# The sample group's part moved from the first to the third group of blocks, with the start reordered

## The chip, the cores and the metric

The kernel runs on one core of a Trainium2 chip. The metric is device time in microseconds (us) of one execution, the median of three runs. A core has five engines that run their own instruction streams and meet at semaphores: TensorE (PE; PEld is its weight load), VectorE (DVE), ScalarE (ACT), GpSimd (POOL) and SyncE (SP). Sixteen DMA engines move data; SP's DMAs stand in the queue that the profile calls q1, ACT's in q10, GpSimd's indirect gathers in q0.

## The reference

One decoder layer is applied to a prompt of 1024 tokens (16 meta tokens ahead of it) and to 8 sample sequences of 4 new tokens (32 rows), with the same weights. The samples attend to a cache of 128 keys and values each, and their pooling goes on from a state of 15 rows.

```python
def layer_step(x, pool_prev, pos0, attn_fn, ...):
    z = x @ w_in                      # pool 512 | q 512 | k 128 | v 128 | two gates of 1024
    g_pool = jax.nn.sigmoid(z[..., OFF_GA:OFF_GB])
    g_attn = jax.nn.sigmoid(z[..., OFF_GB:])
    pool_out, pool_state = pool_mixer(p, pool_prev, pos0, w_pool_mix, pool_scale)
    attn_out, k_state, v_state = attn_fn(q, k, v)
    m = g_pool * (pool_out @ w_up_pool) + g_attn * (attn_out @ w_up_attn)
    x = layer_norm(ALPHA * x + m @ w_out, ln1_g, ln1_b)
    x = layer_norm(ALPHA * x + peer(x, peer_w_query, peer_sub_keys, peer_u, peer_v), ln2_g, ln2_b)

def peer(...):                        # per token: 8 heads, top 16 of 128*128 experts each
    h = gelu(einsum('td,thkd->thk', xb, expert_u[idx]))
    return einsum('thk,thkd->td', gate * h, expert_v[idx])
```

Outputs are the two groups' rows and, for each, the new keys, values and pooling states. The sample states are the caches shifted by the four new rows.

## The kernel before

**Groups and units.** The 8 prompt blocks of 128 tokens are worked in four groups of 1, 2, 2 and 3 blocks (`SIZES`). The meta tokens go with the first group. The 32 sample rows are split: their projections to k, v, pool and q, their attention and their pooling are done in group 0, and from the gates on they go with the third group (`WITH = 2`). A group passes over 58 units of weights (`POS_K`, `POS_V`, four pool tiles, four Q tiles, 16 gate tiles, 8 up, 8 out, 16 queries), each a tile of 128 x 1024 (512 KB). Three tiles of `wring` hold them (`WR = 3`); in the first group six halves of gather tiles help (`FRONT = 9`). A unit's load waits until the unit that used its tile before is done.

**Experts.** Behind its first norm a block is retrieved: queries, scores, top-k, then 128 slots a block (32 for the samples, four rows deep). Each slot gathers 128 rows of 8 KB, the expert's u and v, into one tile of a ring. VectorE makes the dot product with u, ScalarE the gelu and the weight, and the weighted v is summed on PE (matmul with a diagonal, L1103) or on VectorE (L1393); `plan_sums` chooses between them from a table of loads. The ring has 10 tiles (`RING`) and a spare one made of two output rows (`ROWS34`); `JOIN` and `LEAVE` say at which slot a tile comes in and goes. GpSimd issues the gathers in order, each as soon as its tile's last use is summed.

**Order.** Each engine's program is written as parts that yield a place on a common scale, one step per batch of two slots; `interleave` merges them by these places (`Clock`). So units of a later group stand between the sums of earlier blocks on the same engine, and whoever waits holds up what is behind it. SP's program is a plain list of loads: `load_group` goes through the units of a group, and the stores of the sample states stand in it after the second query tile of group 0 (`store_states`).

**The sample data** lie in gather tiles 0 to 3 before the gathers begin: cached keys `kX`, state `sPool`, values `vX`, mask `sMask`, and the scores and probabilities. GpSimd therefore waits for all 13 stores of sample states (`early_out`) before its first gather, and for the sample outputs (`s_o`) before the second.

**The start.** ACT's queue loads small constants; a matmul of the position table (L1120), an add, a store to HBM and a load back in shifted windows (`att<-line_scratch`) make the attention bias, which four matmuls (L1125) turn over. PE does the table before the key tile.

## Time and profile before

| | us |
|---|---|
| median of three runs | 3105.41 (3104.44 to 3107.35) |
| profiled execution | 3107.77 |
| its span | 3105.9 |
| PE busy | 2643.5 |
| DVE busy | 2297.3 |
| ACT busy | 955.6 |
| POOL busy | 1233.7 |

The span runs from the first to the last instruction of the profiled execution; its own time is 1.9 us more. Busy times are summed over the span and say nothing of who waits for whom: the chain of waits and the windows below do. 1255 MB were moved, 1107 MB of them by the gathers.

### The profile page before, as it was taken

How to read it: one execution, taken by the hardware profiler on the slowest of the kernel's cores; microseconds unless marked ns; L12 is line 12 of the kernel's file. 1: busy time of each engine (PE TensorE's matmuls, PEld its weight loads, DVE VectorE, ACT ScalarE, POOL GpSimd, SP SyncE). 2: the span in 40 equal slices, each digit the busy share in tenths (PEclk: the TensorE clock that was granted, in tenths of full speed). 3: DMA queues.
4: the chain of work that ended last, by engine and by line, in shares of the span. 5: the costliest groups of instructions: out<-in, count | busy, mean ns of one | idle time of the engine just before them, and what ended most of it. 6: DMA issues, size and time to landing. Idle time of an engine off the chain costs nothing.

```text
span 3105.9 us, 31170 instructions
## 1 busy us (share of the span) xinstructions
PE 2643.5 (85%) x8204; PEld 1435.9 (46%) x8204; DVE 2297.3 (74%) x4977; ACT 955.6 (31%) x3100; POOL 1233.7 (40%) x1060
## 2 busy tenths in 40 slices
PE   8889999899998888999999879899877777676665
PEld 7866676555544444544444436434322222222222
DVE  2479668888866676888997676788878877666666
ACT  2124323333432232322444221433322322222222
POOL 0123433343443444334444444433454444544542
PEclk9989999999999999999999999999999998988988
DMA  9999999999999999999999999999999999999996
GB/s 284 250 414 417 384 417 419 419 419 419 420 420 418 420 408 412 411 402 414 404 408 380 418 420 420 421 420 418 419 421 421 421 421 422 421 421 422 421 421 259
DMA packets 203654, 1255.14 MB, mean 404 GB/s; under 512 B 31100, under 2 KB 34764, under 8 KB 67920
## 3 DMA queue, kind: packets, MB, share of 16 engines
q0 software_dynamic: 152064, 1107.36, 86.3%
q1 hardware_dynamic: 48656, 139.92, 12.5%
q10 hardware_dynamic: 2760, 5.88, 0.5%
q8 instruction: 68, 1.11, 0.1%
q14 instruction: 106, 0.87, 0.1%
HBM read 1247.39 MB, written 5.79 MB: 403 GB/s over the span
## 4 chain that ended last, share of the span: by engine, by line
DMA 44%; PE 32%; DVE 16%; issue 4%; ACT 2%; DVEq 1%; POOL 1%; ACTq 0%; POOLq 0%
DMA ring<-in_uv,idx 38%; PE acc L1103 15%; PE wide L1084 9%; DVE ring L1382 7%; DMA wring<-in_uv,idx 3%; PE wide L1301 3%; DVE acc_v L1393 2%; DMA wring<-in_w_q 2%; PE wide L1272 2%; DVEq L1366 1%; PE wide L1200 1%; DMA bias<-in_uv,idx 1%; POOL ring L848 1%; PE wide L1182 1%; ACT diag L893 1%
## 5 line engine op out<-in xcount | busy, mean ns | idle before, releaser
L848 POOL DMA_INDIRECT ring<-in_uv,idx x906 | 1054.3, 1164 | 1560.8 <-PE acc L1103 1044.8
L1103 PE MATMUL acc<-ring,diag 128*128 128x512 f32 (+1 forms) x2808 | 1373.1, 630 | 271.7 <-ACT diag L893 258.0
L1382 DVE CUSTOM_DVE_ANT_0 ring<-ring,xb 128x1024 f32<-128x1024 f32 x906 | 1097.0, 1225 | 469.5 <-DMA ring<-in_uv,idx 433.7
L1103 PEld LDWEIGHTS acc<-ring,diag 128*128 128x128 f32 (+1 forms) x2808 | 540.6, 199 | 975.2 <-issue 956.8
L879 ACT ACTIVATE hgelu<-hdot 128x2 f32<-128x2 f32 x528 | 107.2, 203 | 1723.3 <-DVE hdot L1382 1722.8
L1084 PE MATMUL wide<-xm,wring 128*128 128x256 f32 (+5 forms) x2352 | 608.6, 408 | 19.5 <-DMA wring<-in_w_q 18.4
L1084 PEld LDWEIGHTS wide<-xm,wring 128*128 128x128 f32 x2352 | 429.0, 197 | 214.0 <-issue 107.8
L893 ACT ACTIVATE diag<-ident,hw 128x128 f32<-128x128 f32 x813 | 294.3, 396 | 47.9 <-PE acc L1103 5.0
L1393 DVE SCALAR_TENSOR_TENSOR acc_v<-ring,hw,acc_v 128x1024 f32<-128x1024 f32 x204 | 262.1, 1285 | 38.2 <-ACT hw L882 17.9
L882 ACT ACTIVATE hw<-hgelu,gate 128x1 f32<-128x1 f32 x1056 | 253.6, 287 | 37.0 <-issue 0.7
L1301 PE MATMUL wide<-wring,big 128*128 128x256 f32 (+1 forms) x536 | 124.8, 379 | 0.0
L1272 PE MATMUL wide<-inner,wring 128*128 128x256 f32 (+3 forms) x432 | 112.6, 411 | 5.0 <-DMA wring<-in_w_a 5.0
L1301 PEld LDWEIGHTS wide<-wring,big 128*128 128x128 f32 (+1 forms) x536 | 95.2, 180 | 33.9 <-issue 18.5
L1103 PE MATMUL acc<-att,diag 128*128 128x512 f32 (+1 forms) x128 | 69.5, 670 | 42.5 <-ACT diag L893 38.2
L1103 PE MATMUL acc<-bias,diag 128*128 128x512 f32 (+1 forms) x148 | 74.9, 630 | 35.1 <-ACT diag L893 35.1
L1272 PEld LDWEIGHTS wide<-inner,wring 128*128 128x128 f32 x432 | 79.6, 193 | 43.8 <-issue 21.9
L1103 PE MATMUL acc<-xm,diag 128*128 128x512 f32 x100 | 60.3, 735 | 39.5 <-ACT diag L893 39.5
L1382 DVE DVE_READ_ACCUMULATOR2_ANT hdot<- 128x1 f32 x1056 | 86.8, 82 | 0.0
L848 POOL DMA_INDIRECT bias<-in_uv,idx x40 | 48.9, 1223 | 64.1 <-PE acc L1103 53.1
L848 POOL DMA_INDIRECT att<-in_uv,idx x32 | 42.7, 1334 | 76.5 <-PE acc L1103 60.0
L1351 PE MATMUL wide<-wring,qyT 128*128 128x128 f32 x256 | 45.6, 304 | 24.4 <-ACT qyT L1050 24.4
L1382 DVE CUSTOM_DVE_ANT_0 bias<-bias,xb 128x1024 f32<-128x1024 f32 x40 | 49.0, 1226 | 21.9 <-DMA bias<-in_uv,idx 19.9
(242 smaller groups left out, 1992.7 us busy)
## 6 DMA issues: line engine op xcount, KB each, us to landing
wring<-in_w_a SPq DMA_DIRECT2D x141, 512.0 KB, 7.9
wring<-in_w_q SPq DMA_DIRECT2D x64, 576.0 KB, 8.1
ring<-in_uv,idx POOLq DMA_INDIRECT x906, 20.7
ring<-in_w_a SPq DMA_DIRECT2D x27, 512.0 KB, 8.2
out_y_prompt<-xb ACTq DMA_DIRECT2D x7, 512.0 KB, 7.9
att<-in_ln_g SPq DMA_DIRECT2D x4, 512.0 KB, 12.1
att<-in_ln_b SPq DMA_DIRECT2D x4, 512.0 KB, 15.2
xm<-in_xT SPq DMA_DIRECT2D x1, 1536.0 KB, 10.5
```

Source lines behind the costliest of these rows:

```text
L848: pool.indirect_dma_start(slot(s), None, uv, bass.IndirectOffsetOnAxis(ap=idx[:, n % LISTS, j:j + 1], axis=0))\
L879: nc.scalar.activation(hgelu[:, k, :], hdot[:, k, :], ACT.Gelu)
L882: w = nc.scalar.activation(hw[:, k, j:j + 1], hgelu[:, k, j:j + 1], copy, scale=gate[:, n % LISTS, at + j:at + j + 1])
L893: nc.scalar.activation(diag[:, r % DIAGS, 0:width], eye[:, :], copy, scale=hw[:, k, j:j + 1]).then_inc(diag_done, 1)
L1084: m = mm(ps[:, c0:cols(g)], w[:, c, :], x_of(g)[:, c, c0:], start=(c == 0), stop=(c == DC - 1))
L1103: k = mm(acc[0:width, c * 512:(c + 1) * 512], diag[:, r % DIAGS, 0:width], slot(s)[:, D + c * 512:D + (c + 1) * 512], start=(s == first), ...
L1182: m = mm(score_of(i, g)[:, c * 256:(c + 1) * 256], qT[rows, c, first_col(g) + b * P:first_col(g) + (b + 1) * P], kT[rows, b * P:b * P + 2 ...
L1272: m = mm(ps[:, c0:cz], w[:, w0 + c, :], src[:, c, l0:lz], start=(c == 0), stop=(c == 3))
L1301: m = mm(ps, gates(g, 2 * ((k % 2) * 4 + c))[:, a:a + rows], w[:, c, :], start=(k % 2 == 0 and c == 0), stop=(k % 2 == 1 and c == 3))
L1351: m = mm(ps[:, b * P:(b + 1) * P], qyT[:, k % 2, first_col(g) + b * P:first_col(g) + (b + 1) * P], keys, start=True, stop=True)
L1382: V.tensor_tensor_reduce(u, u, x, 1.0, 0.0, ALU.mult, ALU.add, hdot[:, k, j:j + 1])\
L1393: V.scalar_tensor_tensor(acc_v[:, :], slot(s)[:, D:2 * D], hw[:, m % SMALL, BATCH - 1:BATCH], acc_v[:, :], ALU.mult, ALU.add).then_inc(vsl ...
```

## The change

The samples' projections, attention and pooling move from group 0 to group 2, so that group 0 has 16 rows beside its block instead of 48, and group 2 has 32 in every unit. Their data are no longer loaded in the start: SP loads them behind unit loads 2 to 9 of group 2, one or two at a time, and stores the states behind seven gate units. They lie in gather tiles 0 and 1, which leave the ring at slots 142 and 143 and come back at 226 and 216 (`AWAY`, `BACK`); scores and probabilities lie in `att`. GpSimd waits for the stores and the sample outputs only where the two tiles come back. In the start PE does the key tile ahead of the table, the bias matmuls stand behind the first Q tile instead of the second pool tile, SP issues seven weight tiles before it waits for the table (`START`), and the constants of the second norm are loaded at the up projection of group 0. With the samples' work at its new place in its table, `plan_sums` puts 830 sums on PE and 226 on VectorE, where it had 836 and 220.

```diff
-X0 = META + SAMP
-COLS = X0 + GN
+COLS = META + GN
...
-START = 4
+START = 7
-N_CONSTS = 9
+N_CONSTS = 7
...
 def first_col(g):
-    return SAMP if g <= WITH else 0
+    return SAMP if g == WITH else 0
 def x0(g):
-    return X0 if g in (0, WITH) else 0
+    return META if g == 0 else SAMP if g == WITH else 0
...
+        if g == WITH:
+            put(pe, t.attention(-1, 0.02), 10.0, t.attention(-1, 0.96) - t.attention(-1, 0.02))
+            put(dve, t.unit(POS_Q) + 4.8, 5.0)
+            put(dve, t.attention(-1, 0.23), 5.0)
...
+AWAY = {tile: BATCH * int(CLOCKS[WITH].unit(POS_K) - 4) + tile for tile in (0, 1)}
+LEAVE.update(AWAY)
+BACK = {tile: BATCH * int(CLOCKS[WITH].attention(0, 0.0) + 14 - 5 * tile) for tile in (0, 1)}
-JOIN = {ROWS34: RING,
+JOIN = {ROWS34: RING, **BACK,
...
+            def load_samples(k):
+                if k == 0:
+                    for tile in BACK:
+                        wait_slot(sp, LAST_OF[tile], (slot_free, vslot_free))
+                if k < 2:
+                    for c in range(2 * k, 2 * k + 2):
+                        sp.dma_start(sPool[:, c, :, 0:PSTATE], stT[:, c]).then_inc(early_in, 16)
+                elif k == 2:
+                    sp.dma_start(sMask, smask_c).then_inc(early_in, 16)
+                    sp.dma_start(sSink, sink_rows).then_inc(early_in, 16)
+                elif k < 7:
+                    for s in range(2 * (k - 3), 2 * (k - 3) + 2):
+                        sp.dma_start(kX[:, s, 0:WIN], ckT[:, s, :]).then_inc(early_in, 16)
+                elif k == 7:
+                    sp.dma_start(vX, cv_rows).then_inc(early_in, 16)
...
-                    if g == 0 and pos == POS_QRY + 1:
-                        store_states()
+                    if g == WITH and pos <= POS_GATE:
+                        load_samples(pos - WR + 1)
+                    if g == WITH and POS_GATE + 1 <= pos <= POS_GATE + 7:
+                        store_states(pos - POS_GATE - 1)
...
+            def store_states(k):
+                if k == 0:
+                    sp.wait_ge(early_in, 15 * 16)
+                    sp.wait_ge(proj_evac, WITH * PROJ + POS_Q)
+                    sp.dma_start(k_sample, kX[:, :, DSEQ:DSEQ + WIN]).then_inc(early_out, 16)
+                elif k < 5:
+                    c = k - 1
+                    sp.dma_start(pool_sample[:, c], sPool[:, c, :, DSEQ:DSEQ + PSTATE]).then_inc(early_out, 16)
+                else:
+                    for s in range(4 * (k - 5), 4 * (k - 5) + 4):
+                        sp.dma_start(v_sample[s, WIN - DSEQ:WIN, :], sV[DSEQ * s:DSEQ * s + DSEQ])\
+                            .then_inc(early_out, 16)
...
         def _(pool):
-            pool.wait_ge(early_out, 16 * EARLY_STORES)
...
-                    if s == 1:
-                        hold(pool, s_o, 1)
+                    if s == BACK_AT[1]:
+                        hold(pool, s_o, 1)
+                    if s == BACK_AT[0]:
+                        hold(pool, early_out, 16 * EARLY_STORES)
+                        hold(pool, pool_ready, WITH + 1)
...
+                yield CLOCKS[0].unit(POS_UP)
+                act.dma_start(ln2g[:, :], ln2_g.partition_broadcast(P)).then_inc(ln2_in, 16)
+                act.dma_start(ln2b[:, :], ln2_b.partition_broadcast(P)).then_inc(ln2_in, 16)
...
             def position_bias():
-                yield CLOCKS[0].unit(POS_K) - 0.5
+                yield CLOCKS[0].unit(POS_V) - 0.05
...
-                yield CLOCKS[0].unit(POS_POOL + 1) + 0.9
+                yield CLOCKS[0].unit(POS_Q) + 0.9
...
             def sample_attention():
-                count = passes(0)
-                yield CLOCKS[0].attention(count, 0.02)
-                pe.wait_ge(sbias_sb, 1)
+                clock = CLOCKS[WITH]
+                yield clock.attention(-1, 0.16)
                 pe.wait_ge(sq_ready, 1)
```

PE at the start of the program, before the change. A row is so many equal instructions; `xm` holds the input columns, `wring` and `ring` the weight tiles, `acc` the table's result; the last number is the columns.

```order
L1120 MATMUL acc<-ring 8x384
L1084 MATMUL wide<-xm,wring 128x176 x8
L1158 MATMUL wide<-wring,xm 128x128 x8
L1158 MATMUL wide<-wring,xm 32x128 x8
L1158 MATMUL wide<-wring,xm 16x128 x8
L1084 MATMUL wide<-xm,wring 128x176 x8
L1084 MATMUL wide<-xm,ring 128x176 x8
L1125 MATMUL wide<-att,ring 128x512 x4
L1084 MATMUL wide<-xm,ring 128x176 x16
L1132 MATMUL acc<-bias,ring 128x132 x8
L1084 MATMUL wide<-xm,ring 128x160 x24
L1084 MATMUL wide<-xm,wring 128x160 x8
```

And after the change:

```order
L1128 MATMUL wide<-xm,wring 128x144 x8
L1162 MATMUL acc<-ring 8x384
L1202 MATMUL wide<-wring,xm 128x128 x8
L1202 MATMUL wide<-wring,xm 16x128 x8
L1128 MATMUL wide<-xm,wring 128x144 x8
L1128 MATMUL wide<-xm,ring 128x144 x24
L1128 MATMUL wide<-xm,ring 128x128 x8
L1167 MATMUL wide<-att,ring 128x512 x4
L1128 MATMUL wide<-xm,ring 128x128 x8
L1174 MATMUL acc<-bias,ring 128x132 x8
L1128 MATMUL wide<-xm,ring 128x128 x8
L1128 MATMUL wide<-xm,wring 128x128 x12
```

The key tile stands ahead of the table, the units have 32 columns fewer, V has lost its 32-row part, and the four bias matmuls (`att`) have moved from behind two pool tiles to behind the first Q tile. The sample scores, transposes and outputs that followed further down have gone from group 0.

SP at the beginning of the third group, before the change; `in_w_a` are unit weights, `in_xT` the group's input, `in_w_mix` the pooling weights.

```order
L736 DMA wring<-in_w_a 128x1024 x2
L746 DMA xm<-in_xT 128x2432
L736 DMA wring<-in_w_a 128x1024 x2
L740 DMA qyT<-in_w_mix 128x512
L736 DMA wring<-in_w_a 128x1024 x26
```

And after it; `in_stT` is the pooling state, `in_smask` and `in_sink_rows` the mask and the sinks, `in_ckT` the cached keys.

```order
L753 DMA wring<-in_w_a 128x1024 x2
L763 DMA xm<-in_xT 128x2304
L753 DMA wring<-in_w_a 128x1024
L776 DMA ring<-in_stT 128x8x15 x2
L753 DMA wring<-in_w_a 128x1024
L757 DMA qyT<-in_w_mix 128x512
L776 DMA ring<-in_stT 128x8x15 x2
L753 DMA wring<-in_w_a 128x1024
L778 DMA ring<-in_smask 128x576
L779 DMA ring<-in_sink_rows 128x2
L753 DMA wring<-in_w_a 128x1024
L782 DMA ring<-in_ckT 128x128 x2
```

Two loads of the state now stand between the third and the fourth unit's weights, two more ahead of the fifth's, and two of the keys ahead of each of the next.

SP a little further, after the change; before it only unit weights stood here, in one row.

```order
L753 DMA wring<-in_w_a 128x1024 x2
L816 DMA out_k_sample<-ring 1024x1x128
L753 DMA wring<-in_w_a 128x1024
L819 DMA out_pool_sample<-ring 128x8x15
L753 DMA wring<-in_w_a 128x1024
L819 DMA out_pool_sample<-ring 128x8x15
L753 DMA wring<-in_w_a 128x1024
L819 DMA out_pool_sample<-ring 128x8x15
L753 DMA wring<-in_w_a 128x1024
L819 DMA out_pool_sample<-ring 128x8x15
L753 DMA wring<-in_w_a 128x1024
```

The keys' store stands behind the twelfth unit's weights, and one store of the pooling state behind each of the next four.

## Rows read from the trace of the kernel before

**Rows 1.** The page, part 2: rate of DMA, 40 slices of 77.6 us.

```profile
GB/s 284 250 414 417 384 417 419 419 419 419 420 420 418 420 408 412 411 402 414 404 408 380 418 420 420 421 420 418 419 421 421 421 421 422 421 421 422 421 421 259
```

**Rows 2.** Chain that ended last, start: start us, us, engine, tile, line.

```profile
8.02 1.43 PE acc L1120 x2
9.45 4.28 PE wide L1084 x16
13.72 5.39 PE wide L1158 x48
...
34.29 9.78 PE wide L1084 x72
...
46.97 6.45 PE wide L1084 x56
53.41 0.58 PE acc L1216 x6
...
55.76 1.98 PE wide L1084 x16
57.74 0.87 PE wide L1192 x8
...
70.75 0.22 PE wide L1225 x2
...
114.81 0.70 DVE stats L1630
```

**Rows 3.** Timeline, start: start us, us, engine, line, operation [idle before].

```profile
1.19 1.59 SPq L736 DMA_DIRECT2D wring<-in_w_a  x3
...
16.45 0.39 SPq L799 DMA_DIRECT2D att<-line_scratch  x1
...
53.41 1.23 DVE L1553 TENSOR_TENSOR att<-att,aden 128x1024 f32<-128x1024 f32 x1
...
135.23 1.07 POOL L848 DMA_INDIRECT ring<-in_uv,idx  x1 [134.78 <-DVE idx L1675]
```

**Rows 4.** Third group by windows: busy us (instructions) per engine, PEclk, DMA, GB/s.

```profile
750.00:800.00 50.00, 50.00 (x149) 27.35 (x148) 42.75 (x107) 18.97 (x59) 19.83 (x17) 0.97 1.01 420
...
sum 200.00, PE 193.88 PEld 110.64 DVE 168.47 ACT 72.20 POOL 80.31; mean PE 48.47 PEld 27.66 DVE 42.12 ACT 18.05 POOL 20.08
```

**Rows 5.** DMA, 640 to 680 us: queue's MB and share; loads' median landing.

```profile
q0 software_dynamic: 1973, 14.35, 86.4%
...
wring<-in_w_a SPq DMA_DIRECT2D x5, 512.0 KB, 8.6
...
ring<-in_uv,idx POOLq DMA_INDIRECT x13, 20.0
```

**Rows 6.** Tile wring, 0 to 30 us: its loads' landing.

```profile
DMA to landing us min/median/max: 5.5/7.1/8.2
```

**Rows 7.** DMA, 0 to 18 us: the bias window, KB, us to landing.

```profile
att<-line_scratch SPq DMA_DIRECT2D x1, 1024.0 KB, 6.5
```

**Rows 8.** DMA, 25 to 30 us, in which the sample states are loaded.

```profile
DMA packets 4299, 0.62 MB, mean 124 GB/s; under 512 B 4178, under 2 KB 4178, under 8 KB 4299
```

**Rows 9.** DMA, 2168 to 2173 us: queue, packets, MB, share.

```profile
q0 software_dynamic: 273, 1.99, 96.2%
q1 hardware_dynamic: 312, 0.06, 6.5%
```

**Rows 10.** Third group, timeline: SP's loads, and matmuls of units on PE.

```profile
624.78 18.64 SPq L736 DMA_DIRECT2D wring<-in_w_a  x2
...
665.13 3.62 PE L1084 MATMUL wide<-xm,wring 128*128 128x256 f32 x16
...
672.02 1.89 PE L1084 MATMUL wide<-xm,wring 128*128 128x256 f32 x8
...
726.05 2.10 PE L1084 MATMUL wide<-xm,wring 128*128 128x288 f32 x8
...
778.47 2.10 PE L1084 MATMUL wide<-xm,wring 128*128 128x288 f32 x8
```

More of the change, by code:

```diff
@@ L353, in plan_sums @@
         for pos in range(POS_OUT):
-            put(pe, t.unit(pos), 8 * 0.0015 * (n if pos < POS_GATE else wide), 1.5)
+            put(pe, t.unit(pos), 8 * 0.0015 * wide, 1.5)
         for k in range(N_OUT):
@@ L481 @@
 TILE, USE, BEFORE = plan_ring()
+BACK_AT = {tile: TILE.index(tile, at) for tile, at in BACK.items()}
+LAST_OF = {tile: max(s for s in range(BACK[tile]) if TILE[s] == tile) for tile in BACK}
 def interleave(*parts):
@@ L498, in hold, with wait_slot @@
     eng.nop(nofuse=True)
+def wait_slot(eng, s, free):
+    if on_dve(s):
+        eng.wait_ge(free[1], dve_slots(s))
+    else:
+        eng.wait_ge(free[0], pe_slots(s))
 def layer_kernel(nc, xT, w_a, w_q, uv, table, sinks, sink_rows, w_mix, pool_scale,
@@ L1234, in sample_attention @@
                         rows = slice(HD * kv, HD * kv + HD)
-                        out = acc[rows, pair * 32:pair * 32 + 32]
+                        out = wide[0][rows, pair * 32:pair * 32 + 32]
                         for n in range(2):
@@ L1564, in sample_attention @@
             def sample_attention():
-                count = passes(0)
-                yield CLOCKS[0].attention(1, 0.28) + 0.1
-                dve.wait_ge(proj_evac, POS_GATE)
+                clock = CLOCKS[WITH]
+                yield clock.attention(-1, 0.06)
+                dve.wait_ge(early_in, 15 * 16)
+                for t in range(2):
+                    for n in range(2):
+                        mask = sMask[:, t, n * WIN:(n + 1) * WIN]
+                        V.tensor_tensor(mask, sB[:, 0:WIN], mask, ALU.add)
+                    mask = sMask[:, t, 256:288].rearrange("p (s i) -> p s i", s=SEQS)
+                    V.tensor_tensor(mask, sB[:, WIN:WIN + DSEQ].unsqueeze(1).to_broadcast([P, SEQS, DSEQ]), mask, ALU.add)
+                dve.wait_ge(proj_evac, WITH * PROJ + POS_GATE)
                 for s in range(SEQS):
```

160 lines of the change are left out of this document (74 added, 86 removed).

## Prediction

> **What bounds the kernel now.** I read the page first: how much the DMA engines moved, slice by slice. Full rate is about 420 GB/s; it is missed in the first two slices (284 and 250), in the last, and by a little in a few others [rows 1]. So after a start of some 150 us the gathers of expert rows keep the DMA engines full, and the time is roughly that start plus bytes over rate. A change can gain by bringing the first gather forward, and loses by anything it adds to the DMA engines, or holds up in the gathers, later.
>
> Then the chain that ended last, for the start [rows 2]. From 8.0 us to the end of the output projection at 114.8 us it runs on PE almost without a gap: every piece of TensorE work taken from there brings the first gather forward by its own length. What follows (norm, two query tiles, the first top-k) ends with the first index and the gather that waits for it, at 135.23 [rows 3].
>
> Last the third group, which is to take the samples' part. From 650 to 850 us PE is busy for 193.9 of 200 us, in the middle for 50.0 of 50, and DMA moves 420 GB/s there [rows 4]: neither has room. A gather takes 20.0 us from issue to landing [rows 5], of which most is queueing.
>
> **The change, part by part: the start.** A unit of x columns costs in proportion to its columns; a matmul counts as two in the rows, so x16 is one unit.
> - K first. K now waits for the table matmul, which waits until 8.02 for four small loads of ACT's queue, and runs at 9.45 for 4.28 us to 13.72 [rows 2]. The first weight tile lands 5.5 us after its issue at 1.19, at 6.7 [rows 3, 6]. K with 144 columns in place of 176 takes 4.28*144/176 = 3.5, to 10.2; the table matmul after it 1.43, to 11.6. Gain 2.1 us.
> - V loses the samples' third of 48 matmuls: 5.39/3 = 1.8. K aside, the four pool tiles and the four Q tiles lose 32 columns each. The Q tiles took 9.78 with half a gate unit in it, 0.9: 8.9 for four of 160 columns, so 32 columns are 8.9/4*32/160 = 0.44 a unit, and eight units 3.6.
> - Sample scores: from 53.41 to 55.76, 2.35 us. Six transposes: three pieces of 0.22 [rows 2], 0.65.
>
> Sum: 2.1+1.8+3.6+2.35+0.65 = **10.5 us**. The last sample matmuls (L1237) came after the scores that the first index needs, so they don't count. Two covers could be lost. The bias window is issued at 16.45, 7.0 us after the table matmul, and lands 6.5 us later [rows 3, 7]; now 11.6+7.0+6.5 = 25.1. PE reaches the bias matmuls, which are moved behind the first Q tile, at 11.6+3.6+8.0+1.8 = 25.0: a wait of 0.1. And the first transposes need VectorE's probabilities, done at 53.41+1.23 = 54.64 [rows 3], 7.7 us after the scores ended at 46.97 [rows 2]; they run at 57.74, 10.8 us behind the scores, and without the sample scores 8.4 us behind: still covered. The late norm constants and the seven tiles ahead I cost at nothing: PE waits for no weight in the start after the first. If both covers went I would lose 1 us, so 9.5 to 10.5.
>
> **The third group: engines.** PE gets nine units with 32 more columns (9*0.44 = 4.0), V's 1.8, scores 2.35, transposes 0.65 and as many output matmuls as score matmuls, 2.35: about 11 us where it has some 6 idle in 200 [rows 4]. The planner gives some back: it puts 830 sums on PE where it put 836. I take 0 to 8 us, and 2.
>
> **The third group: bytes.** 1.37 MB of caches, state and mask come in and 0.78 MB of state goes out while DMA is full: 2.15 MB at 420 GB/s is 5 us. In the start they lay beside PE.
>
> **The third group: the queue.** This term decides. SP's queue (q1) carries the weight tiles too, in order. The four state loads are made of 60-byte pieces: 4178 packets under 512 bytes stand in the stretch in which they ran [rows 8], 64 for each of 16 DMA engines and load. What do 64 small packets take when the gathers fill the engines? The trace has one such place: the last states' stores at 2160 us. Over 5 us there q1 moved 312 packets, of only 0.06 MB, while q0 moved 273 rows of 8 KB [rows 9]: small or large, a packet of q1 goes about one for one with a gathered row. That is 5*16/312 = 0.26 us for each, so 64 take 17 us. The rate hardly falls; what is behind them in the queue waits.
>
> The Trainium skill (DMA: Bandwidth & Descriptors, "Queues, rings and completion order") says that an engine takes the queues in turn, a packet from each, with typically 9 to 17 descriptors to a packet. Turn by turn the trace agrees (312 to 273); bunches of 9 to 17 it doesn't show. By bunches of 13, 64 would pass in five turns, under 2 us.
>
> First place: SP issues the third unit's weights at 624.78 [rows 10] and now two state loads right behind. The unit's weights land some 8.6 us later, at 633 [rows 5]. Two state loads of 17 us: 667; the next unit's weights 4 us more: 671. PE needs them at 665.13 [rows 10]: 6 us late. Behind them stand the mix weights and two more state loads, 37 us, then the next unit: 712, needed at 672+6. PE waits, and in its queue stand the expert sums that free ring slots. The gathers moved 14.35 MB in 40 us [rows 5], 2.92 us for one of 1.05 MB. A slot goes round in 11*2.92 = 32 us, 12 of them outside DMA (32-20.0); with nine tiles in 26, so some 14 us after PE stops the gathers run dry. Then nothing shares the engines: alone, four state loads passed within 5 us [rows 8]. So the second wait ends after some 16 us: 22 us of PE in all. The stored-up gathers cover 14 of them; about **8 us** are lost (0 to 20).
>
> Second place: k's store and four pool stores, one behind each of five gate units, again 64 packets for each engine. Units follow each other in (778.47-726.05)/4 = 13.1 us [rows 10]; with a store each needs 17+4 = 21. Over five units that is 40 us too much, less a tile's lead of about 15: 25 us of PE, with no reserve left to cover it. Stores too run fast once the gathers are dry, so I take two fifths, **10 us** (0 to 25).
>
> **Sum.** -10.5 + 2 + 5 + 8 + 10 = +14.5 us. The profiled execution took 3107.77 (span 3105.9), 2.4 over the median of the runs, 3105.41. 3107.8+14.5 = 3122.3 in its terms, **3120 us** as a median.
>
> **Rivals.**
> A. As above: SP's queue is too slow for what is put in it and PE waits twice: 3112 to 3138 by the bounds of the two waits, 3120 at the values taken. Chance 0.53.
> B. Little changes on balance. The small packets don't hold up the weights, because they pass in bunches or because a tile's lead of 15 us is enough; the two waits go, and the bytes and a little PE remain: -10.5+5+2 = -3.5, 3102 (3099.2 to 3111.6 with some of a wait). For it: the rate stayed at full while the last states were stored [rows 9]. Against it: the count in the same rows, one for one. The page's bunches would bring this case. Chance 0.26.
> C. Faster: as B, but the bytes too are hidden, since PE at 50.0 of 50 us [rows 4] is what really limits this stretch, and the six sums moved to VectorE pay for the new matmuls: -10.5 to -7, 3095 to 3098. It decides from the point where no weight tile lands after PE asks for it. Against it: gathers in flight for 20 us [rows 5] say that PE keeps ahead and DMA limits. Chance 0.16.
> D. Much slower: with nine tiles each wait goes fully into the gathers, and GpSimd, which now waits for the stores and for the sample outputs before it takes the two tiles back, stands too: 25 more, about 3143. Chance 0.05.
>
> **Numbers.** A measurement of this kernel can tell about 0.2%, 6.2 us: faster is below 3099.2, slower above 3111.6. Faster 0.17 (C and a little of B), same 0.26, slower 0.57. The range leaves out D, and C's lower half: 3097 to 3138.
>
> **What would show it.** Right: first gather at 124.7 (to 126); in the third group waits of PE for wring<-in_w_a at the fourth and fifth unit and again among the gates, state loads that take 15 us or more to land, and a slice there below 400 GB/s. Wrong: no PE wait for weights there and 418 GB/s throughout (B or C), or a first gather later than 128, which would mean that something beside PE bound the start.

## The result, and the profile after

The changed kernel takes 3111.04 us (median of 11 runs, 3108.01 to 3116.46), the kernel before beside it 3105.91 us (11 runs, 3102.39 to 3110.06). The ratio is 1.0018, 95% interval 1.0010 to 1.0025: 5.1 us slower by the medians, clear of no change by the interval, where 14.5 were forecast. The time lies in the range given (3097 to 3138), but just below the 3111.6 us from which the prediction counted it as slower. The profiled execution has a span of 3108.8 us (before: 3105.9).

First the page's rates, slice by slice, to be held against [rows 1]:

```profile
GB/s 296 275 417 413 395 416 419 398 366 419 372 420 420 420 420 413 419 416 419 402 406 389 420 420 420 421 421 416 418 421 421 421 421 422 421 421 422 421 419 270
```

Slices 9 and 11 (622 to 700 and 777 to 855 us), which stood at 419 and 420, are now at 366 and 372. Slice 8 is at 398 in place of 419; a dip there comes back under the ring's two tiles, below. Then the timeline of the start (start us, us, engine, line, operation):

```profile
6.41 3.88 PE L1128 MATMUL wide<-xm,wring 128*128 128x144 f32 x16 [6.41 <-DMA wring<-in_w_a]
10.22 0.81 PE L1162 MATMUL acc<-ring 32*8 32x384 f32 x2
...
24.52 3.60 PE L1167 MATMUL wide<-att,ring 128*128 128x512 f32 x8
...
104.09 0.70 DVE L1673 BATCH_NORM_STATS2 stats<-wide 128x6 f32<-128x512 f32 x1 [7.17 <-PE wide L1342]
...
124.39 1.07 POOL L884 DMA_INDIRECT ring<-in_uv,idx  x1 [123.94 <-DVE idx L1718]
```

The key tile now runs from 6.41 us, as soon as its weights land, and the first gather is issued at 124.39 in place of 135.23 [rows 3]: 10.8 us sooner. In the seven other versions of the changed kernel below it comes 10.3 to 11.1 us sooner. What becomes of that is seen best in the gathers themselves. This table holds, for single gathers, the time at which GpSimd issued them, as a difference to the kernel before (us, from the timelines of one profiled execution each; the columns behind "after" belong to experiments below):

```
gather  after  e_wide_in  e_wide_out  e_wide_both  e_wide_bytes  e_twice_pieces
     0  -10.8      -10.5       -10.3        -10.3         -11.0           -10.9
    48  -15.1      -16.0       -16.3        -15.5         -15.4           -14.9
   132  -13.7      -15.9       -15.8        -15.5         -14.6           -13.7
   168   -7.4       -8.7        -8.6         -8.8          -7.7            -6.3
   180   +5.3       -9.3        +2.6         -8.4          +0.0            +7.7
   216  +16.7       +3.6        +2.3         -1.8         +10.5           +11.4
   264   +6.6       -3.4        -3.1         -6.6          +2.4            +6.9
   408   +7.6       -3.4        -1.6         -6.7          +4.0            +8.2
   984   +4.8       -4.5        -3.6         -7.9          +2.1            +7.3
```

Column "after": the lead grows from 10.8 to some 15 us by gather 48, which I had not forecast, and the third group (gathers 140 to 260) turns it into a lag of 7. That is some 21 us lost there; the forecast had 25. Each column is one execution, and differences of 2 to 3 us in it say little: b_nine_tiles, which takes two tiles away only from gather 142 on, stands 3.2 us behind the kernel before at gather 0 and 1.6 at gather 48.

Where the third group loses it, by windows of 20 us (busy us and instructions of PE, PEld, DVE, ACT and POOL, granted clock, DMA share, GB/s):

```profile
660.00:680.00 20.00, 15.46 (x43) 9.57 (x44) 7.28 (x16) 2.25 (x8) 3.88 (x4) 0.78 0.77 244
780.00:800.00 20.00, 11.06 (x25) 5.76 (x25) 18.56 (x42) 8.28 (x24) 4.39 (x4) 0.79 1.01 350
800.00:820.00 20.00, 20.00 (x62) 11.00 (x61) 10.07 (x29) 6.38 (x19) 7.63 (x7) 0.96 0.84 304
```

And the waits, first in 640 to 680 us (two lines), then in 780 to 800 us (engine, line, what it waited for: us, times, longest):

```profile
POOL xb L884 <- PE acc L1145: 16.5, 1, 16.5
...
PE wide L1128 <- DMA wring<-in_w_a: 12.0, 1, 12.0
...
PE wide L1128 <- DMA wring<-in_w_a: 8.9, 1, 8.9
```

PE is busy for 15.46 and 11.06 of 20 us, and the rates are 244, 350 and 304 where [rows 1, 4] have about 420. PE waits for weights twice, 12.0 and 8.9 us. The first line shows how that reaches the gathers: GpSimd stands 16.5 us for a sum on PE that frees a tile of the ring. At 420 GB/s the bytes missing in the three windows are (176+70+116)*20/420 = 17 us of transfers. From 800 on PE is full again (20.00 of 20) and works off what stood behind the waits.

### The profile page after: what moved, and what is told of

It reads as the page before. It is cut to its first block, busy times and chain, and to the rows that moved or that the text cites. A ratio compares the mean times of both kernels' runs of the same rounds, so it can differ in the third digit from the quotient of the medians.

```text
span 3108.8 us, 31122 instructions
## 1 busy us (share of the span) xinstructions
PE 2631.5 (85%) x8180; PEld 1426.6 (46%) x8180; DVE 2304.8 (74%) x4984; ACT 958.1 (31%) x3096; POOL 1250.9 (40%) x1060
## 4 chain that ended last, share of the span: by engine, by line
DMA 45%; PE 35%; DVE 13%; issue 3%; ACT 2%; DVEq 1%; POOL 1%; ACTq 0%; POOLq 0%; SPq 0%
DMA ring<-in_uv,idx 36%; PE acc L1145 16%; PE wide L1128 11%; DVE ring L1423 5%; DMA wring<-in_w_a 3%; DMA wring<-in_uv,idx 3%; PE wide L1342 2%; PE wide L1313 2%; DVE acc_v L1434 1%; DMA wring<-in_w_q 1%; PE wide L1247 1%; DVEq L1407 1%; DMA xb<-in_uv,idx 1%; DMA bias<-in_uv,idx 1%; PE wide L1227 1%
## 5 line engine op out<-in xcount | busy, mean ns | idle before, releaser
L884 POOL DMA_INDIRECT ring<-in_uv,idx x905 | 1067.8, 1180 | 1532.4 <-PE acc L1145 1001.1
L1145 PE MATMUL acc<-ring,diag 128*128 128x512 f32 (+1 forms) x2780 | 1354.1, 628 | 258.4 <-ACT diag L930 252.2
L1145 PEld LDWEIGHTS acc<-ring,diag 128*128 128x128 f32 (+1 forms) x2780 | 531.9, 198 | 950.4 <-issue 932.5
L1128 PE MATMUL wide<-xm,wring 128*128 128x256 f32 (+4 forms) x2352 | 612.5, 410 | 44.2 <-DMA wring<-in_w_a 27.9
L1434 DVE SCALAR_TENSOR_TENSOR acc_v<-ring,hw,acc_v 128x1024 f32<-128x1024 f32 x210 | 269.7, 1284 | 34.3 <-ACT hw L919 14.8
```

The costliest lines, as they stand in the source:

```text
L884: pool.indirect_dma_start(slot(s), None, uv, bass.IndirectOffsetOnAxis(ap=idx[:, n % LISTS, j:j + 1], axis=0))\
L1128: m = mm(ps[:, c0:cols(g)], w[:, c, :], x_of(g)[:, c, c0:], start=(c == 0), stop=(c == DC - 1))
L1145: k = mm(acc[0:width, c * 512:(c + 1) * 512], diag[:, r % DIAGS, 0:width], slot(s)[:, D + c * 512:D + (c + 1) * 512], start=(s == first), ...
L1434: V.scalar_tensor_tensor(acc_v[:, :], slot(s)[:, D:2 * D], hw[:, m % SMALL, BATCH - 1:BATCH], acc_v[:, :], ALU.mult, ALU.add).then_inc(vsl ...
```

## The experiments

Each median is set against the kernel before, measured beside it in the same session. An interval of a ratio is about 0.09% to either side, 2.8 us, and the ratio isn't simply that of the two medians (for e_wide_out it lies 1.2 us above one, where the medians differ by -0.5 us). So what decides between theories a few us apart is the trace.

| run | base and edit | median us | before beside it | ratio, 95% interval |
|---|---|---|---|---|
| e_wide_both | changed; state loads and stores, k's store as whole rows | 3098.74 | 3105.84 | 0.9980 (0.9971 to 0.9989) |
| e_wide_in | changed; state loads alone as whole rows | 3103.35 | 3105.84 | 0.9995 (0.9986 to 1.0004) |
| e_wide_out | changed; stores alone as whole rows | 3105.60 | 3106.10 | 1.0004 (0.9995 to 1.0013) |
| e_twice_pieces | changed; state loads in twice the pieces | 3110.59 | 3106.10 | 1.0016 (1.0007 to 1.0025) |
| e_act_loads | changed; state loads on ACT's queue | 3114.47 | 3105.54 | 1.0029 (1.0017 to 1.0041) |
| e_wide_bytes | e_wide_both and 4.19 MB more | 3108.84 | 3105.54 | 1.0010 (1.0001 to 1.0019) |
| e_wide_tiles | e_wide_both, two tiles away for less long | 3101.17 | 3106.10 | 0.9985 (0.9976 to 0.9994) |
| b_nine_tiles | before; two tiles away | 3106.62 | 3105.54 | 1.0003 (0.9994 to 1.0012) |
| b_order | before; the start's order alone | 3104.53 | 3105.84 | 0.9999 (0.9990 to 1.0008) |
| b_wide_out | before; stores as whole rows | 3105.54 | 3105.84 | 0.9995 (0.9986 to 1.0004) |
| b_early_stores | before; stores ahead of the up tiles' rest | 3111.49 | 3105.54 | 1.0021 (1.0011 to 1.0030) |
| b_no_out | before; without seven of eight blocks of the samples' output matmuls | 3106.28 | 3106.10 | 1.0000 (0.9991 to 1.0009) |
| b_no_stores | before; without twelve of the thirteen stores | 3105.66 | 3106.42 | 1.0001 (0.9992 to 1.0010) |
| b_neither | before; without both | 3102.56 | 3106.42 | 0.9988 (0.9979 to 0.9997) |

### The small pieces: whole rows in and out

The memory side of the state gets 19 columns in place of 15, so that a load or store of one chunk is one piece of 608 bytes per partition (8 for each DMA engine, not 64).

```diff
-  sp.dma_start(sPool[:, c, :, 0:PSTATE], stT[:, c]).then_inc(early_in, 16)
+  sp.dma_start(sPool[:, c], stT[:, c]).then_inc(st_in, 16)
...
-  sp.dma_start(k_sample, kX[:, :, DSEQ:DSEQ + WIN]).then_inc(early_out, 16)
+  sp.dma_start(k_sample, kX).then_inc(early_out, 16)
...
-  sp.dma_start(pool_sample[:, c], sPool[:, c, :, DSEQ:DSEQ + PSTATE]).then_inc(early_out, 16)
+  sp.dma_start(pool_sample[:, c], sPool[:, c]).then_inc(early_out, 16)
```

**Both** (all three edits, and ACT waits for st_in ahead of the pool tiles):

> The changed kernel with the samples' states padded to 19 columns in memory, so that each of the four state loads and four state stores, and k's store, moves one whole row per partition (608 and 4224 bytes) in place of 60- and 512-byte pieces; ACT waits for the state loads before it writes into them. Nothing else moves. Theory Q (the many small packets in SP's queue hold the weights behind them): the two waits of PE for weights in the third group (12.0 and 8.9 us) go, the DMA rate stays above 410 GB/s from 600 to 860 us, the rise in the gathers' lag over the third group falls from 25 to 10 us or less, and the time is 3094 to 3102 us. Theory E (the samples' PE work, the bytes and the nine tiles of the ring cost it, whatever the packets are): the dip behind 780 us and the lag stay, 3107 to 3112.

**Loads alone** (the first edit):

> The changed kernel with the four state loads alone as whole rows of 608 bytes; the stores stay in small pieces. Theory Q: the first wait (12.0 us at 640 to 680) goes and with it 8 us of missing transfers there, the second (8.9 us at 787 to 796) stays; 3101 to 3106. Theory E: within 2 us of the changed kernel.

**Stores alone** (the second and third):

> The changed kernel with k's store and the four state stores alone as whole rows; the state loads stay in 60-byte pieces. With both as whole rows it took 3098.7, with the loads alone 3103.4, the changed kernel 3111. If the two places add up: the stores are worth 4.6 us here too, 3106 to 3108, the wait of 12.0 us at 652 to 664 stays and the one of 8.9 us at 787 goes. If the gathers' reserve is what decides (the first wait empties it, the second then costs fully): 6 us or more, below 3105.

Measured: 7.1 us under the kernel before with both, 2.5 and 0.5 us under it with one. Against the changed kernel's +5.1 the loads are worth 7.6 us (6.6 where the stores are rows already), the stores 5.6 (4.6 where the loads are). They add up, and theory Q holds for both; theory E is out. (The intervals of the changed kernel and of e_wide_out, and those of e_wide_in and e_wide_both, just overlap, so that the price of the stores rests on both differences and on the waits below.) One part of the expectation failed: the rate was to stay above 410 GB/s from 600 to 860 us, and e_wide_both has 386 from 760 to 780 and 402 from 780 to 800. SP's issues in the changed kernel, by its timeline (x2 are two issues in one row):

```profile
610.16 7.28 SPq L776 DMA_DIRECT2D ring<-in_stT  x2
629.30 8.88 SPq L753 DMA_DIRECT2D wring<-in_w_a  x1
638.22 2.49 SPq L757 DMA_DIRECT2D qyT<-in_w_mix  x1
640.75 20.64 SPq L776 DMA_DIRECT2D ring<-in_stT  x2
661.44 3.31 SPq L753 DMA_DIRECT2D wring<-in_w_a  x1
...
754.66 13.59 SPq L753 DMA_DIRECT2D wring<-in_w_a  x1
```

PE's two waits there, by its timeline:

```profile
664.54 4.18 PE L1128 MATMUL wide<-xm,wring 128*128 128x288 f32 x8 [12.03 <-DMA wring<-in_w_a]
...
796.05 4.18 PE L1128 MATMUL wide<-xm,wring 128*128 128x288 f32 x8 [8.94 <-DMA wring<-in_w_a]
```

And SP's issues in e_wide_both:

```profile
627.57 0.43 SPq L758 DMA_DIRECT2D qyT<-in_w_mix  x1
628.05 0.91 SPq L777 DMA_DIRECT2D ring<-in_stT  x2
636.10 0.33 SPq L754 DMA_DIRECT2D wring<-in_w_a  x1
636.47 0.43 SPq L779 DMA_DIRECT2D ring<-in_smask  x1
```

What PE waits for until 664.54 is the unit that SP issues from 629.30 on, behind the first pair of state loads (610.16). That pair is then still in the queue: its two loads land 32.0 and 50.4 us after their issue, and the unit behind them 35.1 us after its own, at 664.41. The unit of the second wait is issued from 754.66 on, behind the second of the four pool stores, and lands 41.2 us later, at 795.91. The durations show a second effect: the second pair of state loads in pieces keeps SP itself for 20.64 us (640.75 to 661.39), so the next unit's weights aren't even issued before 661.44; as rows two loads take 0.91. That alone cost PE no wait here: its next unit after 664.54 begins without one. The waits answer to the two places: with the loads as rows the only wait of PE for weights from 600 to 860 us is one of 5.1, ending at 783; with the stores as rows it is one of 11.4, ending at 662; with both there is none. The windows of e_wide_both, where the changed kernel had 244, 350 and 304:

```profile
660.00:680.00 20.00, 18.59 (x61) 11.21 (x59) 16.43 (x38) 4.83 (x20) 8.17 (x7) 1.00 1.02 414
780.00:800.00 20.00, 20.00 (x68) 12.01 (x67) 17.74 (x40) 9.10 (x29) 10.61 (x8) 1.00 1.00 402
800.00:820.00 20.00, 20.00 (x57) 10.05 (x56) 15.15 (x49) 7.25 (x22) 8.32 (x9) 1.00 1.01 418
```

This version, e_wide_both, is faster than both kernels.

### How the price depends on the pieces

```diff
-  sp.dma_start(sPool[:, c, :, 0:PSTATE], stT[:, c]).then_inc(early_in, 16)
+  for a, z in ((0, 8), (8, PSTATE)):
+      sp.dma_start(sPool[:, c, :, a:z], stT[:, c, :, a:z]).then_inc(early_in, 16)
```

> The changed kernel with each of the four state loads split into two (8 and 7 of the 15 columns), eight loads of 32- and 28-byte pieces: twice the pieces, the same bytes. By the count of one small packet for one gathered row (275 to 275 in 5 us, 0.29 us each), 64 more pieces for each load and engine are 18.6 us more in the queue for each: the unit behind the first pair comes 37 us later, PE's wait there grows from 12 to 30 us or more (the gathers run dry meanwhile, and then the pieces pass fast), 3120 to 3145. Rival (the price is by bytes or by load, not by piece): within 3 us of the changed kernel.

Measured: 3110.59, as the changed kernel. The expectation fails and the trace says why. First the DMA queues of the changed kernel at 632 to 637 us (queue, packets, MB, share of 16 engines):

```profile
q0 software_dynamic: 277, 2.02, 99.0%
q1 hardware_dynamic: 277, 0.02, 4.0%
```

then this version's at 643.5 to 645.0 us:

```profile
q0 software_dynamic: 75, 0.50, 88.7%
q1 hardware_dynamic: 768, 0.02, 29.0%
```

and its timeline, SP's issues and PE's unit behind the loads:

```profile
610.85 47.26 SPq L777 DMA_DIRECT2D ring<-in_stT  x4
...
664.28 3.85 SPq L777 DMA_DIRECT2D ring<-in_stT  x4
...
667.19 4.18 PE L1129 MATMUL wide<-xm,wring 128*128 128x288 f32 x8 [13.88 <-DMA wring<-in_w_a]
```

While gathers are queued the packets go one for one, 277 to 277 in 5 us, 0.29 us each, 32 bytes as slowly as 60 (112 to 111 from 640 to 642 us). But where the gathers leave a gap, the pieces rush through it: 768 in 1.5 us. This first gap comes before PE stands (from 653.3 on), and the changed kernel has it too; what makes it no run here shows. SP stood for 47 us, from 610.85, so PE's unit was issued only at 658.15, but with the pieces ahead of it gone it landed at 667.05, 2.6 us later than in the changed kernel, and PE waited 13.9 us. By then the gathers had run dry, and the second four loads took 3.85 us to issue. So I read a ceiling out of these two runs: the price is set by where the gathers run thin, and not by the number of pieces. The prediction said as much of the second wait; the expectation named it, but gave it too little weight.

```diff
-  if k < 2:
-      for c in range(2 * k, 2 * k + 2):
-          sp.dma_start(sPool[:, c, :, 0:PSTATE], stT[:, c]).then_inc(early_in, 16)
...
   wait_slot(act, LAST_OF[0], (slot_free, vslot_free))
+  for c in range(4):
+      act.dma_start(sPool[:, c, :, 0:PSTATE], stT[:, c]).then_inc(early_in, 16)
```

> The changed kernel with the four state loads, in the same 60-byte pieces, issued by ACT in its own queue at the third group's key unit in place of SP. Theory O (it is the order in SP's queue: weights stand behind the pieces): no PE wait for weights at 640 to 680 us, though the loads may take 40 us and more to land; VectorE may then wait for them at the pooled windows; 3102 to 3107. Rival P (4096 small packets take the engines' turns from all queues): the weights still come late, or the rate falls below 400 GB/s there, 3109 to 3113.

Measured: 8.9 us over the kernel before, worse than either theory had it. The timeline, ACT and PE:

```profile
634.02 0.39 ACTq L974 DMA_DIRECT2D ring<-in_stT  x1
...
634.43 21.24 ACTq L974 DMA_DIRECT2D ring<-in_stT  x3
655.72 0.20 ACT L984 ACTIVATE ring<-wide 128x32 f32<-128x32 f32 x1 [21.12 <-issue]
...
657.46 5.99 PE L1144 MATMUL acc<-ring,diag 128*128 128x512 f32 x8 [16.82 <-ACT diag L927]
```

and the queues at 640 to 645 us:

```profile
q0 software_dynamic: 197, 1.43, 69.9%
q1 hardware_dynamic: 168, 0.58, 29.5%
q10 hardware_dynamic: 196, 0.01, 2.8%
```

Theory O is right about the weights: q1 is served beside q10, about packet for packet (197, 168, 196), and PE waits for no weight there (a wait of 5.8 us is left at the stores, ending at 796.56). But now ACT stands in the issue of the last three loads (21.24 us), PE waits 16.82 us for the diagonals that ACT makes, and the gathers run dry all the same. So it is the issuing engine that stands, SP in one case and ACT in the other.

### The bytes

```diff
+  for k in range(2):
+      act.dma_start(spare_rows[2 * c + k], cache_v).then_inc(states_out, 16)
   act.wait_ge(st_in, 64)
```

> The version with whole rows in and out, plus eight copies of the V cache (0.52 MB each, 4.19 MB in all) from memory to unused memory, issued by ACT at the third group's four pool units. Theory by bytes (DMA is full there, every byte costs): 4.19 MB at 420 GB/s, 10 us over the version with whole rows (3098.7): 3107 to 3110. Rival (the third group has hidden room, and what the samples' 2.15 MB cost is something else): under 4 us, below 3103.

Measured: 3.3 us over the kernel before, where e_wide_both is 7.1 under: 10.4 us for 4.19 MB, 2.5 us per MB. ACT stood for none of it: its eight issues took 0.50 to 0.61 us each. The theory by bytes holds; at this rate the samples' 2.15 MB cost 5.3 us, an estimate.

### The ring's two tiles

```diff
+  AWAY = {0: 142, 1: 143}
+  LEAVE.update(AWAY)
+  BACK = {0: 226, 1: 216}
+  JOIN = {ROWS34: RING, **BACK,
```

> The kernel before with ring tiles 0 and 1 out of use for the same gathers as in the changed kernel (from gathers 142 and 143 to 226 and 216), and nothing else moved: no sample work, no transfer. In the version with whole rows the DMA rate fell to 372, 360 and 396 GB/s from 580 to 610 us, just after the tiles are taken. Theory R (nine tiles are a price of their own): the same fall there, 3 us lost for good, some 3 to 5 us more lag until the tiles are back at 810 us; 3108 to 3111. Rival: that dip comes from the plan's moved sums, and nine tiles cost nothing: 3105 to 3106.

```diff
-  AWAY = {tile: BATCH * int(CLOCKS[WITH].unit(POS_K) - 4) + tile for tile in (0, 1)}
+  AWAY = {tile: BATCH * int(CLOCKS[WITH].unit(POS_K) - 1) + tile for tile in (0, 1)}
-  BACK = {tile: BATCH * int(CLOCKS[WITH].attention(0, 0.0) + 14 - 5 * tile) for tile in (0, 1)}
+  BACK = {tile: BATCH * int(CLOCKS[WITH].attention(0, 0.0) + 10 - 4 * tile) for tile in (0, 1)}
```

> The version with whole rows in and out, with ring tiles 0 and 1 taken six gathers later (148 and 149) and given back eight and six gathers sooner (218 and 210). The kernel before with the same tiles away and no samples took 3106.6, 1 us more than without. If nine tiles cost 3 us here, where PE has the samples' work too, a part of it comes back: 3096 to 3098; if they cost 1 us or less: within 1 us of 3098.7.

Windows of 10 us in b_nine_tiles:

```profile
590.00:600.00 10.00, 10.00 (x39) 6.75 (x38) 9.62 (x34) 6.15 (x16) 1.89 (x2) 1.00 0.98 390
600.00:610.00 10.00, 10.00 (x37) 6.41 (x36) 9.34 (x30) 3.68 (x16) 1.87 (x2) 1.00 0.95 340
```

and in e_wide_tiles:

```profile
590.00:600.00 10.00, 10.00 (x35) 5.85 (x34) 9.06 (x29) 1.98 (x8) 3.29 (x3) 1.00 1.02 419
600.00:610.00 10.00, 6.42 (x22) 3.42 (x21) 8.79 (x18) 3.83 (x16) 2.39 (x2) 1.00 1.02 424
```

The first shows the dip that theory R expects, 390 and 340 GB/s without any sample work; the second shows it gone with the tiles taken later. In time neither moved anything: 1.1 us over the kernel before, and 3101.17 against 3098.74 with intervals that overlap. So neither theory R's 3108 nor a price of nothing is shown. The lag that nine tiles bring is mostly given back when the tiles return (in b_nine_tiles the gathers' difference goes from 2.2 us at gather 132 to 8.0 at 180 and back to 3.7 at 264, 2.0 at 984). I put their price at 0 to 2 us, as an estimate.

### Where the lead of 15 us comes from

```diff
-START = 4
+START = 7
...
-                yield CLOCKS[0].unit(POS_K) - 0.5
+                yield CLOCKS[0].unit(POS_V) - 0.05
```

(with the bias matmuls and the norm's constants late as in the changed kernel)

> The kernel before with the start's order alone: the key tile ahead of the table matmul, seven weight tiles ahead of the table's store, bias matmuls behind the first Q tile, the second norm's constants late; the samples stay in the first group. By the sum of the prediction K's move gives 2.1 us less what its 32 sample columns take (0.8), or the full gap of 1.4 us and more: first gather at 133 to 134, 3103 to 3105. Rival: the sample bias on VectorE, 2.4 us later, or the line's load becomes what the start waits for, and nothing is gained, 3105 to 3107.

Measured: the first gather 1.0 us sooner, 1.3 us in the median, which its interval can't tell from nothing. So most of the 10.8 us goes with the samples' work that left the start.

What the first gather doesn't show is the 4 us gained between gathers 0 and 48. In the kernel before two things stand between the second and the third query tile: on PE the samples' output matmuls, in SP's queue the thirteen stores. Each was changed alone:

```diff
-  sp.dma_start(k_sample, kX[:, :, DSEQ:DSEQ + WIN]).then_inc(early_out, 16)
+  sp.dma_start(k_sample, kX).then_inc(early_out, 16)
...
-  sp.dma_start(pool_sample[:, c], sPool[:, c, :, DSEQ:DSEQ + PSTATE]).then_inc(early_out, 16)
+  sp.dma_start(pool_sample[:, c], sPool[:, c]).then_inc(early_out, 16)
```

> The kernel before with k's store and the four state stores alone as whole rows; nothing else moves. In the kernel before these stand in SP's queue ahead of the query tiles, and from 110 to 125 us the DMA engines moved only 111 GB/s. Theory Q: the query tiles land in about 5 us in place of 11.5, the gathers behind the first come 4 to 5 us sooner, and the time falls by 3 to 5 us, to 3101 to 3103. Theory E (what lies behind the first index in the start is hidden by the top-k work): within 1 us of the kernel before.

```diff
-  if g == 0 and pos == POS_QRY + 1:
+  if g == 0 and pos == POS_UP + 1:
       store_states()
```

> The kernel before with the thirteen stores of the samples' states (small pieces as they are) issued behind the second up tile of the first group in place of behind the second query tile. In the kernel before SP issues them from 109.55 to 117.5 us, and the third query tile behind them only at 118.19; with whole rows that stayed so (118.72) and nothing was gained. Theory S (SP's issuing time, some 8.5 us for thirteen issues, holds the query tiles): the third query tile is issued before 112 us, PE's wait of 3.6 us at 140 to 143 goes, gathers 13 to 120 come 3 to 4 us sooner, 3101 to 3103. Rival: the lag comes from the last sample matmuls and VectorE's work behind the first index, and nothing is gained, 3105 to 3106.

```diff
   for kv in range(2):
+      if (pair, kv) != (3, 1):
+          continue
```

> The kernel before with seven of the eight blocks of the samples' output matmuls (L1237, L1239) left out of the first group, so that the samples' attention output isn't computed; nothing else moves. In the kernel before these stand on PE from 125.50 to 130.85 us, between the second and the third query tile's work, and the granted clock falls behind them. Theory M (they hold the query tiles and through them the gathers from the eleventh on, though not the first): first gather unchanged within 1 us, gathers 13 to 120 come 3 to 5 us sooner, 3100 to 3103. Rival L (the query tiles wait for their loads, which SP issues late, whatever PE does before): PE's wait of 3.6 us behind 140 us grows by as much, nothing gained, 3104 to 3106.

Measured: nothing gained by any. With whole rows the query tiles land in 3.7 us (10.4 before, median over 110 to 130 us), but the third is still issued at 118.72: its load waits until PE has done the unit that used its tile, which ends at 118.70 there, and not for the stores. The early stores cost 6 us at their new place: they hold the up tiles' weights there, PE waits 3.6 us (to 91.78), and behind the wait its granted clock is at the lower level, 0.50 of 2.4 GHz from 92 to 96 us; the mean from 90 to 100 is 0.66 (1.00 in the kernel before). And without the matmuls PE stands as long as they took. The wait and the window of b_early_stores:

```profile
PE wide L1272 <- DMA wring<-in_w_a: 3.6, 1, 3.6
```

```profile
90.00:100.00 10.00, 8.22 (x47) 8.25 (x48) 1.55 (x6) 0.00 (x0) 0.00 (x0) 0.66 0.96 356
```

and PE's third query tile in the timeline of b_no_out:

```profile
132.46 4.91 PE L1084 MATMUL wide<-xm,wring 128*128 128x128 f32 x24 [5.84 <-DMA wring<-in_w_q]
```

The third query tile begins at 132.46 after a wait of 5.84 us for its weights. What the stores hold is their landing. The third tile's load, by the DMA view of the first us behind its issue (KB, us to landing), in the kernel before and in b_no_stores (below):

```profile
wring<-in_w_q SPq DMA_DIRECT2D x1, 576.0 KB, 12.7
wring<-in_w_q SPq DMA_DIRECT2D x1, 576.0 KB, 3.5
```

Behind the stores it lands at 130.84, just when the output matmuls end (130.85); without them at 122.11, and PE is then still at the matmuls. That made a theory: each of the two hides the other. Its test left out the stores, and the stores and the matmuls (the diff of b_no_out above, and this one):

```diff
-  sp.dma_start(k_sample, kX[:, :, DSEQ:DSEQ + WIN]).then_inc(early_out, 16)
-  for s in range(SEQS):
-      sp.dma_start(v_sample[s, WIN - DSEQ:WIN, :], sV[DSEQ * s:DSEQ * s + DSEQ]).then_inc(early_out, 16)
-  for c in range(4):
-      sp.dma_start(pool_sample[:, c], sPool[:, c, :, DSEQ:DSEQ + PSTATE]).then_inc(early_out, 16)
+  sp.dma_start(v_sample[0, WIN - DSEQ:WIN, :], sV[0:DSEQ]).then_inc(early_out, 16)
```

> The kernel before with twelve of the thirteen stores of the samples' states left out (k, the four states and seven of the eight v pieces are not written); nothing else moves. Theory J (the stores in SP's queue and the output matmuls on PE hold the third query tile to the same time, 131 us, and each hides the other): the third query tile's load is issued before 112 us and lands early, PE still begins it at about 131, gathers 48 to 120 within 1.5 us of the kernel before; 3104 to 3106. Rival: the stores' bytes or their place alone were what held it, 3 to 5 us sooner, 3100 to 3103.

> The kernel before with those twelve stores and seven of the eight blocks of the samples' output matmuls left out. Theory J: PE begins the third query tile at 126 to 127 us, without a wait of more than 1 us, gathers 48 to 120 come 3.5 to 5.5 us sooner though the first doesn't move, and the time falls by 3 to 5 us, to 3101 to 3103. Rival: a third thing holds it (the evacuation of the queries by ACT, the top-k on VectorE), and the gathers stay within 1.5 us.

Measured: without the stores nothing (0.8 us, far inside the interval), without both 3.9 us faster, interval 0.9 to 6.5 us. Two details of the expectations failed. The third tile's load was not issued before 112 us but at 118.58. And in b_neither gathers 48 to 120 came 2.0 to 2.7 us sooner, not 3.5 to 5.5, with the first gather 2.7 later; measured from their first gather they gained about 5 (b_nine_tiles, unchanged there, 1.6 at gather 48). PE's timeline up to the third query tile, in the kernel before (the matmuls' last row, the tile):

```profile
130.43 0.42 PE L1239 MATMUL acc<-ring 32*64 32x32 f32 x2
130.98 5.18 PE L1084 MATMUL wide<-xm,wring 128*128 128x128 f32 x24
```

in b_neither:

```profile
127.74 0.49 PE L1349 MATMUL wide<-wring,qyT 128*128 128x128 f32 x2 [0.37 <-ACT qyT L1046]
...
128.73 2.94 PE L1080 MATMUL wide<-xm,wring 128*128 128x128 f32 x24
```

and in the changed kernel:

```profile
114.37 0.49 PE L1392 MATMUL wide<-wring,qyT 128*128 128x128 f32 x2 [0.37 <-ACT qyT L1094]
114.69 3.10 PE L1128 MATMUL wide<-xm,wring 128*128 128x128 f32 x24
```

Between the second query tile's last two matmuls and the third tile there were 5.4 us of output matmuls (125.50 to 130.85), the last of them and the 24 behind them slower (5.18 us); in the other two the 24 follow within 0.5 us (in b_neither behind the one block that is left) and take 2.94 and 3.10. That is what theory J says: two covers lay over each other, and only taking both away, as the change does, uncovers the gain. Its size, 3.9 us, is known no better than its interval.

## Why the prediction was right, and where it was wrong

The forecast, 14.5 us, is 9.4 too high. Its mechanism came, by its own signs: first gather at 124.39 (124.7 forecast), PE waiting for weights behind the state loads and again among the gates, state loads that took 22.7 to 50.4 us to land, slices of 366 and 372 GB/s. What failed are two terms of the sum: one put at nothing, which measured 3.9 us, and the 10 us of the second place, which measured 4.6 to 5.6.

Of the sums, two don't come out. Rival A's 3112 to 3138 is said to follow from the bounds of the two waits; 0 to 20 and 0 to 25 give 3102 to 3147. The measured 3111.04 lies in that, but just below A's span as written and inside B's (up to 3111.6 with some of a wait). And D's 25 us more than 3120 is 3145, not 3143.

**The start: right for what it counted, and a term left out.** Forecast 9.5 to 10.5 us, measured 10.8 at the first gather, with K at 6.41 (forecast 6.7) and no cover lost: the bias matmuls begin at 24.52 without a wait. The step that failed is "The last sample matmuls (L1237) came after the scores that the first index needs, so they don't count". They don't hold the first gather; they do hold the third query tile, and with the stores beside them the gathers behind the first: 3.9 us (0.9 to 6.5), by b_neither. I had taken the first index for the end of the start, while the gathers behind it wait for later query tiles.

**The small packets: the rule right.** One for one with a gathered row, 0.26 us a piece, measured 0.29. The Trainium skill's bunches of 9 to 17 descriptors (DMA: Bandwidth & Descriptors, "Queues, rings and completion order") are not seen with these pieces; its turn by turn is, also with three queues. By bunches the prediction had rival B, 3102.

**First place: the loss right, its working not.** Forecast 8 us lost (0 to 20): two waits of 6 and 16, less 14 until the gathers run dry. Measured 6.6 to 7.6 from one wait of 12.0: the second pair of loads went while the gathers were already dry. By the forecast's cover of 14 a wait of 12 would have cost nothing. In the trace the gathered rows run out at 663, some 11 us after PE stops, and none moves until 672: GpSimd issues the next gather only at 671.22, 6.7 us after PE has begun again, since sums must first free a tile. The forecast had left out this way back, so that its 8 us came out is luck.

**Second place: mis-sized.** Forecast 10 us (0 to 25) from 25 us of PE waiting, measured 8.9 us of waiting and 4.6 to 5.6 us lost. The step is "with a store each needs 17+4 = 21. Over five units that is 40 us too much, less a tile's lead of about 15". That lets the pieces go one for one through all five units, 105 us. In the trace the five stores' pieces are through in some 80 (720 to 805): one for one until 775 (283 beside 284 packets of gathers from 770 to 775), then in rushes where the gathers run thin (635 packets beside 81 from 784 to 786), as in e_twice_pieces. The prediction knew that stores run fast once the gathers are dry, but took it off the loss alone, by its two fifths, and not off the wait. How much of the 15 us of lead there was no run here shows.

**Bytes and engines.** Bytes: forecast 5, and 5.3 by the rate of e_wide_bytes. Engines and the ring: forecast 2 (0 to 8); by the sum below 2.3 are left for them, nine tiles included. No run measured the samples' work on the engines by itself.

**The sum.** Forecast -10.5+2+5+8+10 = 14.5. Measured: -10.8 (first gather) -3.9 (b_neither) +12.2 (both kinds of pieces, 5.1+7.1) +5.3 (bytes) leaves 5.1-2.8 = 2.3 for engines and tiles. The miss of 9.4 is the 3.9 that were left out and 10-4.6 = 5.4 in the second place, nearly all of it. The sum closes because the 2.3 are what is left over; each difference of medians in it carries some 2.8 us, so that they come out near the forecast 2 is partly luck.

**The rivals.** B (the pieces don't hold the weights) and C (as B, and the bytes hidden) are out as accounts of what happened, by the waits and by e_wide_bytes. D's extra, 25 us for tiles and GpSimd standing, didn't come: the tiles are put at 0 to 2 us. What e_wide_both measures, 3098.74, is about what B gave (3102) with the left-out 3.9 taken off.

## What to carry to other kernels

Count a transfer by its packets for each DMA engine as well as by its bytes: on full queues 64 pieces of 60 bytes held the queue as long as 64 gathered rows of 8 KB, and laying the state out so that a partition's part is one piece turned a change that cost 5 us into one that gains 7. Where something is taken out of a place, look for what else holds that place until the same time: here removing either of two covers alone measured as nothing, and both together as 4 us. And read a gain at the start not from the first gather alone but also from later ones, such as the fiftieth here, where the lead has settled.

## What the hardware showed that I had not expected

- An engine that issues loads in many small pieces stands in the issue of the later ones, with no semaphore to wait for: SP 20.64 us for two, ACT 0.39 us for the first and 21.24 for the next three, against 0.91 us for two loads of whole rows. What stands behind it on that engine stands too: weights on SP, the diagonals that PE needs on ACT. I take it that the queue was full; no run here shows how much it holds.
- Two queues that both had work were served packet for packet, gathered rows of 8 KB beside small pieces: 277 to 277 in 5 us with 60-byte pieces, 112 to 111 in 2 us with 32-byte ones, and nearly so with three queues, 197, 168 and 196.
- Where one queue had a gap the other took it at once: 398 packets, nearly all pieces of 60 bytes, in 1.5 us (643.5 to 645.0 in the changed kernel), and 768 of at most 32 bytes in the same 1.5 us of e_twice_pieces.
- The start differs by up to 3 us from one profiled execution to the next where nothing in it was changed (the first gather came 3.2 us later in b_nine_tiles than in the kernel before; in b_neither, where work was only taken out, 2.7 later), so a lead below that can't be read from one trace.
